# Gate and up of a gated feed-forward by seven half-size block products instead of eight, block sums on GpSimd

## The chip, the cores and the metric

One core of one Trainium2 chip runs the whole program. The metric is device time in microseconds (us). The engines are TensorE (PE, with its weight loads as PEld), VectorE (DVE), ScalarE (ACT), GpSimd (POOL) and SyncE (SP), which issues the loads of weights.

## What is computed

The reference is a stack of four layers on 512 tokens of width 1024, all in float32: two layers with a mixer, a cross attention to a memory, and a gated feed-forward; then two layers with another mixer and a feed-forward of squared ReLU. The change is in the gated one:

```python
D_FF = -(-(8 * D_MODEL) // (3 * 256)) * 256          # 2816
def swiglu_ffn(x, w_gate, w_up, w_down):
    return (jax.nn.silu(x @ w_gate) * (x @ w_up)) @ w_down
...
for l in range(DEPTH):                                # DEPTH = 2
    ...
    y = swiglu_ffn(x, ffn_wg[l], ffn_wu[l], ffn_wd[l])
    x = layer_norm(ALPHA * x + y, ln_ffn_g[l], ln_ffn_b[l])
```

## The kernel before

Activations lie feature-major: `xs` holds eight tiles (k) of 128 features by 512 tokens. A float32 product is made of three single-pass products: each operand is split into a high part (fp32r, written by ACT) and the rest (written by DVE), and `mm3` adds high*high, high*rest and rest*high in a PSUM bank. So every matmul of a product stands three times, each with its own weight load.

Weights come as units of 128 x 2048 floats (1 MB), in the order of their use. SP loads a unit into one of the two halves of `w_raw` when DVE has finished with the unit before in it; ACT writes the high part (`split_hi`, into `w_hi`) when PE is done with the unit before in that half, and DVE the rest (`split_lo`, into `w_lo`). Each engine has its own instruction stream, in order; all order between engines is by semaphores. PE runs the units in turn.

A gated feed-forward has 11 chunks of 256 hidden features. A chunk has three units: gate, up and down. `chunks("ffn0", ...)` and `chunks("ffn1", ...)` do on PE: gate and up of chunk 0; then ten times gate and up of chunk c (96 matmuls of 512 tokens) and down of chunk c-1 (48 of 512); then down of chunk 10. Gate and up each fill two PSUM banks (0 to 3) over eight k. ACT drains the gate with SiLU into `sil`, DVE multiplies it by up (`fh`), ACT and DVE split the product into `fhh` and `fhl` (L1622, L2258), and PE's down reads these. Down has eight output tiles, in banks 4 to 7 in turn; DVE adds each to `xs` (L2160), and tile m+4 can start only when tile m has been added. GpSimd computes nothing in this part. `scale_residual` (eight scalings of `xs` on DVE) stands beside the gate of chunk 0.

In all the trace's rows the matmuls have line 710 (`mm`), and the splits of units lines 1483 (ACT) and 2074 (DVE).

Of the kernel before, what the change touches and what calls it, by code (L numbers as in the profile page):

```python
# [30 lines left out]
KT = D // P  # L31
# [95 lines left out]
def plan_banks():  # L127
# [116 lines left out]
    def ups(name, tag, c, gated):  # L244
        f = []
        if gated:
            f += [((name, tag, "g", 0), 0, None), ((name, tag, "g", 1), 1, c)]
            c += 1
        b = 2 if gated else 2 * (side(UNITS[name]) ^ (tag != "first"))
        return f + [((name, tag, "u", 0), b, None), ((name, tag, "u", 1), b + 1, c)]  # L250
# [4 lines left out]
    def chunks(name, gated):  # L255
        c, k = UNITS[name], 2 if gated else 1
        for f in ups(name, "first", c, gated):
            fill(*f)
        c += k
        trips = LOOP_TRIPS[gated]  # L260
        loop(trips, 2 * (k + 1), ups(name, 0, c, gated) + downs(name, 0, c + k)
             + ups(name, 1, c + k + 1, gated) + downs(name, 1, c + 2 * k + 1))
        c += trips * 2 * (k + 1)
        if not gated:
            for f in ups(name, "late", c, gated) + downs(name, "late", c + k):
                fill(*f)
            c += k + 1
        for f in downs(name, "last", c):
            fill(*f)
# [6 lines left out]
    for l in range(2):  # L276
# [29 lines left out]
        chunks(f"ffn{l}", True)  # L306
# [13 lines left out]
    chunks("mlp0", False)  # L320
# [10 lines left out]
    chunks("mlp1", False)  # L331
# [3 lines left out]
LOOP_TRIPS = {True: (FFN_CHUNKS - 1) // 2, False: (MLP_CHUNKS - 2) // 2}  # L335
# [9 lines left out]
SO_FIRST = 12  # L345
plan_banks()


def slot(c):
    return (c + sum(s < c for s in SPARE)) % 2  # L350
# [30 lines left out]
class Seen:  # L381
# [14 lines left out]
SIGNALS = [  # L396
    "first_hi", "first_lo",
# [26 lines left out]
def build(nc, x, mem, params, consts, table, w_gk2, sinks, w, out):  # L424
    scratch = nc.dram_tensor("rel_scratch", [16, P, 384], F32, kind="Internal").ap()
    with ExitStack() as ctx:
# [8 lines left out]
        raw_loaded = [new_sem(f"raw_loaded{s}") for s in range(2)]  # L435
# [44 lines left out]
        sum_x = sb(ctx, "sum_x", [P, T])  # L480
        sum_q = sb(ctx, "sum_q", [P, T])
# [9 lines left out]
        meml = sb(first, "meml", [P, KT, MEM], F32R)  # L491
        mk = sb(first, "mk", [P, KT, MEM])
        vl0 = sb(alias, "vl0", [P, MT * D], F32R)
        alias.close()
# [18 lines left out]
        values_lo = [vl0, vl1]  # L513
        mv1 = sb(first, "mv1", [P, MT * D])
# [7 lines left out]
        sil = sb(ffn_mem, "sil", [P, 2, T])  # L522
        fh = sb(ffn_mem, "fh", [P, 2, T])
        fhh = sb(ffn_mem, "fhh", [P, 2, 2, T], F32R)
        fhl = sb(ffn_mem, "fhl", [P, 2, 2, T], F32R)
        ffn_mem.close()
# [28 lines left out]
        gb = sb(gla_mem, "gb", [P, HEADS, T])  # L555
        gk = sb(gla_mem, "gk", [P, HEADS, T])
# [7 lines left out]
        low_mem = ExitStack()  # L564
        glr_hi = sb(low_mem, "glr_hi", [P, KT * P], F32R)
        glr_lo = sb(low_mem, "glr_lo", [P, KT * P], F32R)
        low_mem.close()
# [15 lines left out]

        banks = [ctx.enter_context(nc.psum_tensor(f"bank{b}", [P, T], F32)) for b in range(8)]
# [4 lines left out]
        def wait_full(eng, key, i=None):  # L589

            b, _, _, unit, n, per = FILL[key]
            if unit is None:
                eng.wait_ge(bank_full[b], at(i, per, n))
            else:
                eng.wait_ge(unit_used, at(i, per, unit + 1))
# [24 lines left out]
        def last_down_keys(name):  # L620
            return [(name, "last", "d", m) for m in range(KT)]

        chunk_base = {"ffn0": 0, "ffn1": FFN_CHUNKS, "mlp0": 2 * FFN_CHUNKS, "mlp1": 2 * FFN_CHUNKS + MLP_CHUNKS}
        gated = {"ffn0": True, "ffn1": True, "mlp0": False, "mlp1": False}
# [5 lines left out]
        def _(sp):  # L630
            def load(s, n):
                sp.dma_start(w_raw[:, s, :], w[n, :, :]).then_inc(raw_loaded[s], 16)
# [10 lines left out]
            load(1, 1)  # L643
            with sp.Fori(1, N_UNITS // 2) as i:
                for s in range(2):
                    sp.wait_ge(w_lo_ready, i * 2 + (s - 1))
                    sp.dma_start(w_raw[:, s, :], w[bass.ds(i * 2 + s, 1), :, :].rearrange("a p n -> p (a n)"))\
                      .then_inc(raw_loaded[s], 16)
            if N_UNITS % 2:
                sp.wait_ge(w_lo_ready, N_UNITS - 2)  # L650
                load(0, N_UNITS - 1)
# [8 lines left out]
        def _(pool):  # L660
# [20 lines left out]
            pool.wait_ge(unit_used, UNITS["ffn0"] + 1)  # L681
            const(window[:, :, :, :].rearrange("p a g t -> p (a g t)"), "window", window_loaded)
            pool.wait_ge(unit_used, UNITS["glr"])
# [7 lines left out]
            pool.wait_ge(unit_used, UNITS["mlp0"])  # L691
            const(kk[0:33, 0, 0:384], "onehot", onehot_loaded, 33)
            wait_drained(pool, ("vec", 0))
            for g in range(8):
                heads = slice(2 * g, 2 * g + 2)
                pool.wait_ge(unit_used, UNITS["mlp0"] + 3 + 2 * g)
                pool.dma_start(scratch[heads, :, :], vt[heads, 0:384].unsqueeze(1).broadcast_to([2, P, 384])).then_inc(vec_stored, 16)
            pool.wait_ge(vec_stored, 8 * 16)
            for g in range(8):
                pool.wait_ge(unit_used, UNITS["mlp0"] + 20 + g)  # L700
# [5 lines left out]
        def _(pe):  # L706
# [29 lines left out]
            def feature_unit(stage, j, src=xtile, n=T, ready=None):  # L736

                c = UNITS[stage] + j
                if c:
                    pe.wait_ge(w_lo_ready, c + 1)  # L740
# [10 lines left out]
            def last_unit(stage, j, src=xtile):  # L751

                c = UNITS[stage] + j
                pe.wait_ge(w_lo_ready, c + 1)
# [6 lines left out]
            def token_half(stage, p, half, src, tiles):  # L761

                c = UNITS[stage] + 2 * p + half
                pe.wait_ge(w_lo_ready, c + 1)
# [93 lines left out]
            def keep_array_busy(key, c):  # L858

                pe.wait_ge(w_hi_ready, c + 1)  # L860
# [188 lines left out]
            def out_tiles(l, tiles):  # L1049
# [3 lines left out]
                if tiles[0] == 0:  # L1053
                    pe.wait_ge(w_lo_ready, c + 1)
# [53 lines left out]

            def chunks(name, ready):


                U, base, gate = UNITS[name], chunk_base[name], gated[name]
                hh, hl = (fhh, fhl) if gate else (mhh, mhl)
                src = xtile if gate else ytile
                k_ = 2 if gate else 1

                def up(tag, c, i=None, ready=None):
                    for which in ("g", "u") if gate else ("u",):
# [3 lines left out]
                        for k in range(KT):  # L1122
                            if ready:
                                ready(k)
# [1763 lines left out]
```

## Time and profile before

| | |
|---|---|
| time, median of 3 runs | 2422.66 us (2421.19 to 2422.84) |
| span of the profiled execution | 2419.9 us |
| its time around the span | not shown on the page; the median is 2.8 us above the span |
| PE busy | 2386.0 us, 99% |
| DVE, ACT, GpSimd busy | 1448.5, 873.7, 22.7 us |

The profile is one execution with hardware timestamps. Its page gives each engine's busy time and the chain of work that ended last; the trace behind it gives single instructions in order of time, groups of instructions with mean duration (one line per shape), busy times within stretches, and the DMA issues with their time to landing. A matmul's duration overlaps that of the next one, so what a matmul costs is read from the distance between two starts, not from its mean duration.

### The profile page before, as it was taken

How to read it: one execution, taken by the hardware profiler on the slowest of the kernel's cores; microseconds unless marked ns; L12 is line 12 of the kernel's file. 1: busy time of each engine (PE TensorE's matmuls, PEld its weight loads, DVE VectorE, ACT ScalarE, POOL GpSimd, SP SyncE). 2: the span in 40 equal slices, each digit the busy share in tenths (PEclk: the TensorE clock that was granted, in tenths of full speed). 3: DMA queues.
4: the chain of work that ended last, by engine and by line, in shares of the span. 5: the costliest groups of instructions: out<-in, count | busy, mean ns of one | idle time of the engine just before them, and what ended most of it. 6: DMA issues, size and time to landing. Idle time of an engine off the chain costs nothing.

```text
span 2419.9 us, 28651 instructions
## 1 busy us (share of the span) xinstructions
PE 2386.0 (99%) x11134; PEld 1944.4 (80%) x11134; DVE 1448.5 (60%) x1994; ACT 873.7 (36%) x1230; POOL 22.7 (1%) x39
## 2 busy tenths in 40 slices
PE   8999999999999999999999999999999999999998
PEld 7887888888887887888887786888888777888886
DVE  6997646444446846444446725565566776665566
ACT  4455445222223834322223625422122465222122
POOL 0000000000000000000000000000000000000000
PEclk9999999999999999999999999999999999999999
DMA  5222312322222211222222220233333211222221
GB/s 183 105 101 92 122 35 105 114 104 88 103 88 103 77 64 70 105 97 94 97 94 102 77 105 35 83 109 118 120 112 120 87 53 64 93 96 95 104 90 66
DMA packets 38811, 228.06 MB, mean 94 GB/s; under 512 B 8837, under 2 KB 8917, under 8 KB 12496
## 3 DMA queue, kind: packets, MB, share of 16 engines
q1 hardware_dynamic: 31680, 219.17, 25.3%
q0 software_dynamic: 7056, 7.86, 1.3%
q8 instruction: 52, 0.85, 0.1%
q14 instruction: 23, 0.19, 0.0%
HBM read 221.71 MB, written 5.24 MB: 94 GB/s over the span
## 4 chain that ended last, share of the span: by engine, by line
PE 86%; DVE 7%; ACT 5%; issue 1%; DMA 1%; SPq 0%; DVEq 0%; ACTq 0%
PE bank L710 85%; DVE w_lo L2074 2%; ACT w_hi L1483 1%; DMA w_raw<-weights_in 1%; ACT xs L1564 1%; ACT xh L1502 1%; DVE xl L2089 1%; DVE cacc L2310 1%; PE bank L1414 1%; DVE xs L2204 0%; DVE xs L2184 0%; ACT pr L1806 0%; DVE sum_x L2096 0%; DVE sum_q L2103 0%; DVE xs L2160 0%
## 5 line engine op out<-in xcount | busy, mean ns | idle before, releaser
L2074 DVE TENSOR_TENSOR w_lo<-w_raw,w_hi 128x2048 fp32r<-128x2048 f32 x200 | 458.2, 2291 | 372.7 <-ACT w_hi L1483 372.6
L710 PE MATMUL bank<-xh,w_hi 128*128 128x512 f32 x1408 | 553.6, 393 | 13.3 <-DVE w_lo L2532 6.7
L710 PE MATMUL bank<-xl,w_hi 128*128 128x512 f32 x1408 | 548.9, 390 | 0.0
L710 PE MATMUL bank<-xh,w_lo 128*128 128x512 f32 x1408 | 548.8, 390 | 0.0
L1483 ACT ACTIVATE w_hi<-w_raw 128x2048 fp32r<-128x2048 f32 x200 | 381.6, 1908 | 400.1 <-PE bank L710 394.1
L2160 DVE TENSOR_TENSOR xs<-xs,bank 128x512 f32<-128x512 f32 x448 | 294.5, 684 | 102.1 <-PE bank L710 101.1
L710 PEld LDWEIGHTS bank<-xh,w_hi 128*128 128x128 f32 x1408 | 264.8, 188 | 77.2 <-DVE w_lo L2532 6.7
L710 PEld LDWEIGHTS bank<-xh,w_lo 128*128 128x128 f32 x1408 | 264.8, 188 | 55.4
L710 PEld LDWEIGHTS bank<-xl,w_hi 128*128 128x128 f32 x1408 | 265.0, 188 | 54.3 <-issue 0.5
L710 PE MATMUL bank<-yh,w_hi 128*128 128x512 f32 x576 | 227.2, 394 | 0.4 <-DVE w_lo L2074 0.3
L710 PE MATMUL bank<-yl,w_hi 128*128 128x512 f32 x576 | 224.3, 389 | 0.0
L710 PE MATMUL bank<-yh,w_lo 128*128 128x512 f32 x576 | 224.2, 389 | 0.0
L710 PE MATMUL bank<-mhh,w_hi 128*128 128x512 f32 x512 | 199.2, 389 | 0.0
L710 PE MATMUL bank<-mhl,w_hi 128*128 128x512 f32 x512 | 199.2, 389 | 0.0
L710 PE MATMUL bank<-mhh,w_lo 128*128 128x512 f32 x512 | 199.2, 389 | 0.0
L1622 ACT ACTIVATE mhh<-mh 128x512 fp32r<-128x512 f32 x64 | 39.5, 633 | 312.9 <-DVE mh L2254 312.9
L2249 DVE TENSOR_TENSOR mh<-bank,rstd 128x512 f32<-128x512 f32 x64 | 43.7, 691 | 173.8 <-PE bank L710 173.8
L710 PE MATMUL bank<-fhh,w_hi 128*128 128x512 f32 x352 | 136.9, 389 | 0.0
L710 PE MATMUL bank<-fhl,w_hi 128*128 128x512 f32 x352 | 136.9, 389 | 0.0
L710 PE MATMUL bank<-fhh,w_lo 128*128 128x512 f32 x352 | 136.9, 389 | 0.0
L710 PEld LDWEIGHTS bank<-yh,w_hi 128*128 128x128 f32 x576 | 108.1, 188 | 28.5 <-issue 6.6
L710 PEld LDWEIGHTS bank<-yh,w_lo 128*128 128x128 f32 x576 | 108.1, 188 | 22.9
(299 smaller groups left out, 2868.3 us busy)
## 6 DMA issues: line engine op xcount, KB each, us to landing
w_raw<-weights_in SPq DMA_DIRECT2D x204, 1024.0 KB, 4.8
rel_scratch<-vt POOLq DMA_DIRECT2D x8, 384.0 KB, 19.9
bias<-rel_scratch POOLq DMA_DIRECT2D x8, 256.0 KB, 3.2
y_out<-xs SPq DMA_DIRECT2D x8, 256.0 KB, 2.2
xs<-x_in SPq DMA_DIRECT2D x3, 512.0 KB, 8.7
mk<-mem_in POOLq DMA_DIRECT2D x1, 1024.0 KB, 7.3
window<-consts_in POOLq DMA_DIRECT2D x1, 576.0 KB, 6.4
xs<-x_in SPq DMA_DIRECT2D x2, 256.0 KB, 4.5
```

The source lines that it names most:

```text
L710: return pe.matmul(dst, a, b, start=start, stop=stop)
L1414: last = pe.transpose(bank(key)[:, s_ * P:(s_ + 1) * P], pv[:, s_ * P:(s_ + 1) * P], ident[:, :])
L1483: act.activation(w_hi[:, slot(c), :], w_raw[:, c % 2, :], ACT.Copy).then_inc(w_hi_ready, 1)
L1502: give(act.activation((xh if dst is None else dst)[:, k, :], src, ACT.Copy, **kw), "x_hi")
L1564: give(act.activation(xs[:, k, :], xs[:, k, :], ACT.Identity, scale=col(f"{param}_g{l}", k), bias=col(f"{param}_b{l}", k)), "xn_ready")
L1622: give(act.activation(hh[:, chunk % 2, m, :], src, ACT.Copy), "hh_ready")
L2074: dve.tensor_tensor(w_lo[:, slot(c), :], w_raw[:, c % 2, :], w_hi[:, slot(c), :].bitcast(F32), ALU.subtract)\
L2089: return dve.tensor_tensor(l, src, h, ALU.subtract)
L2160: free(dve.tensor_tensor(xs[:, k, :], xs[:, k, :], bank(key)[:, :], ALU.add), key)
L2249: free(dve.tensor_tensor(hid[:, chunk % 2, m, :], bank(key)[:, :], rstd[:, :], ALU.mult), key)
L2310: ins = dve.scalar_tensor_tensor(a, u, wj, a, ALU.mult, ALU.add)
```

## The change

Chunk 0 of each gated layer stays as it was. For chunks 1 to 10, gate and up are computed by Strassen's scheme: the contraction (1024 features) is cut into halves (low, high), the tokens into halves (early, late) and the 256 hidden features into halves. Instead of eight products of such blocks there are seven, of sums of blocks. One product takes gate and up together (u = 0, 1 in the two halves of one bank): 2 x 4 k x 3 = 24 matmuls with 256 tokens, so 168 for a chunk. The order of the products is 2, 5, 1, 4, 3, 7, 6 of the token operands.

- Sums of weight blocks (five for each chunk, each 128 x 1024 floats) and of token blocks (five for each layer) are made by GpSimd, into two buffers (`sums`, `sq`) in turn; a sum waits until DVE has made the rest of the sum before last (`sum_parts`).
- ACT and DVE split seven half units for each chunk (`unit_part`, 128 x 1024 each) in place of two whole ones. The parts of products lie in a ring of three: the part of product n+3 can be written only when product n is done.
- Products come out of PSUM by three ACT copies and six DVE additions into `gu`, and two subtractions between quarters of it (`from_copies`). SiLU and the product with up then run in `gu`.
- The gate and up units of chunk c+1 overwrite `w_raw` when the last sum of chunk c has been made. Down units have a raw buffer of their own, and a single place in `w_hi` and `w_lo` (the other place is part of the ring): `split_hi` of a down unit waits until the down before it is done on PE.
- SP's loads and the gated layers' code are written out instead of looped. `scale_residual` moves behind the seventh part of chunk 1. The host packs gate and up weights in quarters (`quartered`).

```diff
--- before.py
+++ after.py
...
+        def ring(name, c, j):
+            g = (PRODUCTS * (c - 1) + j) % RING
+            if g == 0:
+                return ring_hi[:, :], ring_lo[:, :]
+            a, s = slice((g - 1) * UNIT // 2, g * UNIT // 2), 1 - W_SLOT[UNITS[name] + 1]
+            return w_hi[:, s, a], w_lo[:, s, a]
+
+        def quadrant(q):
+            return w_raw[:, :, q * T:(q + 1) * T]
+
+        def sum_of(key):
+            return (sq if SUM[key] % 2 else sums)[:, :, :]
...
+            for n in range(2, N_UNITS):
+                before = RAW_BEFORE[n]
+                if before in PAIRED:
+                    name, c = PAIRED[before]
+                    sp.wait_ge(sem["sum_made"], SUM[name, c, PRODUCTS - 1] + 1)
+                    sp.wait_ge(sem["part_lo"], PART[name, c, 1] + 1)
+                elif n in (down_unit("ffn0", 0), down_unit("ffn1", 0)):
+                    sp.wait_ge(unit_used, nth(n - 4) + 1)
+                else:
+                    sp.wait_ge(w_lo_ready, nth(before) + 1)
+                load(n)
...
+            def sum_parts(name, key, a, b, op):
+                t = SUM[key]
+                if t >= 2:
+                    pool.wait_ge(sem["part_lo"], SUM_PART[t - 2] + 1)
+                pool.tensor_tensor(sum_of(key), a, b, op).then_inc(sem["sum_made"], 1)
...
+            def gated_sums(name, norms):
+
+                pool.wait_ge(sem["xn_ready"], norms * KT)
+                sum_tokens(name, 2, (low, late), (high_, late), ALU.add)
+                sum_tokens(name, 5, (low, early), (high_, early), ALU.add)
+                sum_tokens(name, 1, (low, early), (high_, late), ALU.add)
+                for c in range(1, FFN_CHUNKS):
+                    for n in (UNITS[name] + 3 * c - 1, UNITS[name] + 3 * c):
+                        pool.wait_ge(raw_loaded[RAW_SLOT[n]], 16 * RAW_COUNT[n])
+                    sum_parts(name, (name, c, 2), quadrant(0), quadrant(3), ALU.add)
+                    sum_parts(name, (name, c, 3), quadrant(2), quadrant(0), ALU.subtract)
+                    if c == 1:
+                        sum_tokens(name, 7, (high_, early), (high_, late), ALU.subtract)
+                        sum_tokens(name, 6, (low, late), (low, early), ALU.subtract)
+                    sum_parts(name, (name, c, 4), quadrant(1), quadrant(3), ALU.subtract)
+                    sum_parts(name, (name, c, 5), quadrant(2), quadrant(3), ALU.add)
+                    sum_parts(name, (name, c, 6), quadrant(0), quadrant(1), ALU.add)
...
+                def product(c, j, s):
+                    key = (name, "p", c, j)
+                    pe.wait_ge(sem["part_lo"], PART[name, c, j] + 1)
+                    wait_free(pe, key)
+                    wh, wl = ring(name, c, j)
+                    h, l = operand(s)
+                    for u in range(2):
+                        for k in range(KT // 2):
+                            a = slice(u * T + k * P, u * T + (k + 1) * P)
+                            last = mm3(bank(key)[:, u * 256:(u + 1) * 256], (wh[:, a], wl[:, a]), (h[:, k, :], l[:, k, :]),
+                                       k == 0, k == KT // 2 - 1)
+                    full(last, key)
+
+                whole("g", UNITS[name], ready)
+                whole("u", UNITS[name] + 1)
+                for c in range(1, FFN_CHUNKS):
+                    for j, s in enumerate((2, 5, 1, 4, 3, 7, 6)):
+                        product(c, j, s)
+                    down(name, c - 1, down_unit(name, c - 1), c - 1)
+                down(name, FFN_CHUNKS - 1, down_unit(name, FFN_CHUNKS - 1), FFN_CHUNKS - 1)
...
+                if c - 1 in DOWNS and c not in DOWNS and i is None:
+                    act.wait_ge(unit_used, nth(c - 1))
+                elif W_BEFORE[c] is not None:
+                    act.wait_ge(unit_used, at(i, per, nth(W_BEFORE[c]) + 1))
+                act.activation(w_hi[:, slot(c), :], raw(c), ACT.Copy).then_inc(w_hi_ready, 1)
...
+                def unit_part(c, j):
+                    key = (name, c, j)
+                    g = PRODUCTS * (c - 1) + j
+                    if g >= RING:
+                        before = (g - RING) // PRODUCTS + 1, (g - RING) % PRODUCTS
+                        wait_full(act, (name, "p", *before))
+                    elif g:
+                        act.wait_ge(unit_used, nth(U) + (own_slot == W_SLOT.get(U)))
+                    if j >= 2:
+                        act.wait_ge(sem["sum_made"], SUM[key] + 1)
+                        src = sum_of(key)
+                    else:
+                        for n in (U + 3 * c - 1, U + 3 * c):
+                            act.wait_ge(raw_loaded[RAW_SLOT[n]], 16 * RAW_COUNT[n])
+                        src = quadrant(3 * j)
+                    give(act.activation(ring(name, c, j)[0].rearrange("p (u n) -> p u n", u=2), src, ACT.Copy), "part_hi")
...
+                def gate(c, f):
+
+                    for j in ((3, 5), (4, 6))[f]:
+                        wait_drained(act, (name, "p", c, j))
+                    g = gu[:, gate_side(name, c), f, :]
+                    give(act.activation(g, g, ACT.Silu), "sil_ready")
...
+                for c in range(1, FFN_CHUNKS):
+                    act.wait_ge(sem["h_ready"], 2 * (base + c))
+                    product_out(c, 0, 0, late)
+                    unit_part(c, 3)
+                    split_hi(down_unit(name, c - 1))
+                    if c == 1:
+                        act.wait_ge(unit_used, nth(U + 1) + 1)
+                        for s in (7, 6):
+                            token_part(s)
+                    product_out(c, 1, 1, early)
+                    unit_part(c, 4)
+                    product_out(c, 2, 0, early)
+                    unit_part(c, 5)
+                    unit_part(c, 6)
+                    if c + 1 < FFN_CHUNKS:
+                        unit_part(c + 1, 0)
+                        unit_part(c + 1, 1)
+                    gate(c, 0)
+                    if c + 1 < FFN_CHUNKS:
+                        unit_part(c + 1, 2)
+                    gate(c, 1)
+                    for m in range(2):
+                        hidden(c, m)
+                split_hi(down_unit(name, FFN_CHUNKS - 1))
...
+                def from_copies(c):
+
+                    for j in range(3):
+                        wait_drained(dve, (name, "p", c, j))
+                    steps.step(dve.tensor_tensor(quarter(1, late), quarter(0, early), quarter(0, late), ALU.subtract))
+                    steps.step(dve.tensor_tensor(quarter(0, early), quarter(0, early), quarter(1, early), ALU.subtract))
+
+                def add_to_two(c, j, first, second):
+
+                    wait_full(dve, (name, "p", c, j))
+                    steps.wait()
+                    steps.step(add_product(c, j, *first))
+                    free(add_product(c, j, *second), (name, "p", c, j))
+
+                def add_to_one(c, j, f, t, behind):
+                    wait_full(dve, (name, "p", c, j))
+                    steps.wait()
+                    wait_drained(dve, (name, "p", c, behind))
+                    free(add_product(c, j, f, t), (name, "p", c, j))
...
+                for s in (2, 5, 1):
+                    token_part(s)
+                for j in range(RING):
+                    unit_part(1, j)
+                for m in range(2):
+                    first_hidden(m)
+                for m in range(2):
+                    rest_of_hidden(0, m)
+                for c in range(1, FFN_CHUNKS):
+                    unit_part(c, 3)
+                    if c == 1:
+                        for s in (7, 6):
+                            token_part(s)
+                    split_lo(down_unit(name, c - 1))
+                    unit_part(c, 4)
+                    from_copies(c)
+                    unit_part(c, 5)
+                    add_to_two(c, 3, (0, early), (0, late))
+                    unit_part(c, 6)
+                    if c == 1:
+                        dve.wait_ge(sem["sum_made"], SUM[name, "x", 6] + 1)
+                        scale_residual()
+                    add_to_two(c, 4, (1, early), (1, late))
+                    if c + 1 < FFN_CHUNKS:
+                        unit_part(c + 1, 0)
+                    add_to_one(c, 5, 0, early, 3)
+                    if c + 1 < FFN_CHUNKS:
+                        unit_part(c + 1, 1)
+                    add_to_one(c, 6, 1, late, 4)
+                    hidden(c, 0)
+                    down(c - 1, range(0, 2))
+                    hidden(c, 1)
+                    down(c - 1, range(2, 3))
+                    if c + 1 < FFN_CHUNKS:
+                        unit_part(c + 1, 2)
+                    down(c - 1, range(3, 5))
+                    rest_of_hidden(c, 0)
+                    down(c - 1, range(5, 6))
+                    rest_of_hidden(c, 1)
+                    down(c - 1, range(6, KT))
+                split_lo(down_unit(name, FFN_CHUNKS - 1))
+                keys = last_down_keys(name)
+                for k in range(KT):
+                    add(k, keys[k])
+                    sums_between(k, keys, True)
```

## Rows read from the trace of the kernel before

**Rows 1.** The page: busy times, and granted clock of PE over 40 slices.

```profile
PE 2386.0 (99%) x11134; PEld 1944.4 (80%) x11134; DVE 1448.5 (60%) x1994; ACT 873.7 (36%) x1230; POOL 22.7 (1%) x39
...
PEclk9999999999999999999999999999999999999999
```

**Rows 2.** Chain that ended last, one stretch: start, us, what.

```profile
999.96 66.19 PE bank L710 x292
```

**Rows 3.** Windows: two passes of the loop of chunks.

```profile
core 0: us, PE busy (x) PEld busy (x) DVE busy (x) ACT busy (x) POOL busy (x), PEclk, DMA share, GB/s
1000.00:1065.24 65.24, 65.24 (x289) 54.03 (x288) 29.19 (x30) 15.92 (x14) 0.00 (x0) 1.00 0.27 97
```

**Rows 4.** Timeline of PE, 512 tokens: start, us; first and last of 24.

```profile
391.66 0.39 PE L710 MATMUL bank<-xh,w_hi 128*128 128x512 f32 x1
...
396.87 0.40 PE L710 MATMUL bank<-xh,w_lo 128*128 128x512 f32 x1
```

**Rows 5.** Timeline of PE, 256 tokens: first and last of 47.

```profile
145.40 0.28 PE L710 MATMUL bank<-meml,w_hi 128*128 128x256 f32 x1
...
150.92 0.28 PE L710 MATMUL bank<-memh,w_lo 128*128 128x256 f32 x1
```

**Rows 6.** Groups of DVE: busy us, mean ns; idle before.

```profile
line engine op names shapes xcount | busy us, mean ns | idle before us <-releasers
L2074 DVE TENSOR_TENSOR w_lo<-w_raw,w_hi 128x2048 fp32r<-128x2048 f32 x200 | 458.2, 2291 | 372.7 <-ACT w_hi L1483 372.6
L2160 DVE TENSOR_TENSOR xs<-xs,bank 128x512 f32<-128x512 f32 x448 | 294.5, 684 | 102.1 <-PE bank L710 101.1
...
L2258 DVE TENSOR_TENSOR fhl<-fh,fhh 128x512 fp32r<-128x512 f32 x44 | 28.6, 690 | 2.2
L2247 DVE TENSOR_TENSOR fh<-sil,bank 128x512 f32<-128x512 f32 x44 | 28.3, 685 | 118.4 <-PE bank L710 111.2 <-issue 7.2
...
L2224 DVE TENSOR_SCALAR xs<-xs 128x512 f32<-128x512 f32 x16 | 5.5, 422 | 0.0
...
L2522 DVE TENSOR_TENSOR vl<-mv,vh 128x1024 fp32r<-128x1024 f32 x4 | 4.9, 1218 | 0.0
```

**Rows 7.** Groups of ACT.

```profile
L1483 ACT ACTIVATE w_hi<-w_raw 128x2048 fp32r<-128x2048 f32 x200 | 381.6, 1908 | 400.1 <-PE bank L710 394.1 <-DMA w_raw<-weights_in 6.0
...
L1622 ACT ACTIVATE fhh<-fh 128x512 fp32r<-128x512 f32 x44 | 27.1, 633 | 190.8 <-DVE fh L2247 190.8
L1488 ACT ACTIVATE sil<-bank 128x512 f32<-128x512 f32 x44 | 26.3, 598 | 165.6 <-PE bank L710 163.8
...
L1801 ACT ACTIVATE vh<-mv 128x1024 fp32r<-128x1024 f32 x4 | 4.2, 1047 | 0.0
```

**Rows 8.** Groups of GpSimd: its largest compute operation and a smallest.

```profile
L667 POOL MEMSET ones<- 128x128 f32 x1 | 0.2, 205 | 0.0
...
L666 POOL MEMSET eps<- 128x1 f32 x1 | 0.1, 98 | 0.3 <-POOLq L2878 0.3
```

**Rows 9.** DMA issues: count, KB each, median us to landing.

```profile
w_raw<-weights_in SPq DMA_DIRECT2D x204, 1024.0 KB, 4.8
```

**Rows 10.** Windows within one load: DMA share, GB/s.

```profile
core 0: us, , PEclk, DMA share, GB/s
1012.00:1013.00 1.00, 1.00 0.76 221
1013.00:1014.00 1.00, 1.00 0.92 369
1014.00:1015.00 1.00, 1.00 0.94 393
1015.00:1016.00 1.00, 1.00 0.16 66
```

**Rows 11.** Timeline of DVE in one chunk.

```profile
1013.59 0.69 DVE L2160 TENSOR_TENSOR xs<-xs,bank 128x512 f32<-128x512 f32 x1 [0.67 <-PE bank L710]
...
1029.63 2.29 DVE L2074 TENSOR_TENSOR w_lo<-w_raw,w_hi 128x2048 fp32r<-128x2048 f32 x1 [9.07 <-ACT w_hi L1483]
```

**Rows 12.** Waits: who waited for whom.

```profile
ACT w_hi L1483 <- PE bank L710: 394.1, 60, 9.4
DVE w_lo L2074 <- ACT w_hi L1483: 372.6, 121, 9.4
```

More of the change, by code:

```diff
@@ L642, in _ @@
                 sp.dma_start(xs[:, 2 * c:2 * c + 2, :], x[:, 2 * c:2 * c + 2, :]).then_inc(x_loaded[c + 1], 16)
[L643 to L651, printed above, removed]
+            load(1)
+            for n in range(2, N_UNITS):
[9 more added lines that the diff above has]
+                load(n)
             for k in range(KT):
@@ L1107, in cross_attention, with down @@
                 return step
+            def down(name, tag, c, chunk, i=None, per=0):
+                hh, hl = (fhh, fhl) if name[:3] == "ffn" else (mhh, mhl)
+                pe.wait_ge(w_lo_ready, at(i, per, nth(c) + 1))
+                pe.wait_ge(sem["h_ready"], at(i, 4, 2 * (chunk_base[name] + chunk) + 2))
+                for m in range(KT):
+                    key = (name, tag, "d", m)
+                    wait_free(pe, key, i)
+                    for k in range(2):
+                        last = mm3(bank(key)[:, :], weights(c, k * D + m * P, P),
+                                   (hh[:, chunk % 2, k, :], hl[:, chunk % 2, k, :]), k == 0, k == 1)
+                    full(last, key)
@@ L1133, in down @@
-                def down(tag, c, chunk, i=None):
-                    pe.wait_ge(w_lo_ready, at(i, per, c + 1))
-                    pe.wait_ge(sem["h_ready"], at(i, 4, 2 * (base + chunk) + 2))
-                    for m in range(KT):
-                        key = (name, tag, "d", m)
-                        wait_free(pe, key, i)
-                        for k in range(2):
-                            last = mm3(bank(key)[:, :], weights(c, k * D + m * P, P),
-                                       (hh[:, chunk % 2, k, :], hl[:, chunk % 2, k, :]), k == 0, k == 1)
-                        full(last, key)
@@ L1146, in chunks @@
+                per = 4
                 up("first", U, ready=ready)
-                c = U + k_
-                with pe.Fori(0, trips) as i:
+                c = U + 1
+                with pe.Fori(0, MLP_TRIPS) as i:
                     up(0, c, i)
-                    down(0, c + k_, 0, i)
-                    up(1, c + k_ + 1, i)
-                    down(1, c + 2 * k_ + 1, 1, i)
-                c += trips * per
-                if not gate:
-                    up("late", c)
-                    down("late", c + k_, 2 * trips)
-                    c += k_ + 1
```

482 lines of the change are left out of this document (304 added, 178 removed).

## Prediction, made before the change was run

> **What bounds the kernel.** I read the page first. PE is busy 99% of the span at the full granted clock, DVE 60%, ACT 36%, GpSimd 1% [rows 1]. The chain of work that ended last is nothing but PE in the middle of a gated layer: one piece of 66.19 us with 292 matmuls [rows 2]. The windows over one pass of the loop of chunks (two chunks) say the same: PE has no gap in 65.24 us, DVE works 29.19 and ACT 15.92 [rows 3]. The waits are those of ACT for PE and of DVE for ACT, not of PE [rows 12], and DVE stands idle for 9.07 us ahead of one split [rows 11]. So only PE's matmuls count before, and whatever delays PE afterwards counts in full.
>
> What does a matmul cost? Its duration (0.39 us) overlaps the next one's. The distance of starts is what counts: 24 matmuls of 512 tokens start from 391.66 to 396.87, which is 5.21 / 23 = 0.2265 us [rows 4]; 47 of 256 tokens from 145.40 to 150.92, which is 5.52 / 46 = 0.120 us [rows 5]. Half the tokens cost 53%, not 50%: about 13 ns of each matmul does not scale. A chunk of 144 matmuls of 512 then takes 32.62 us, and two of them 65.24, as in [rows 3].
>
> **What PE saves.** Gate and up of a chunk: 96 x 0.2265 = 21.74 us before, 168 x 0.120 = 20.16 after. One eighth less arithmetic would be 2.7 us; the fixed part of 72 more matmuls takes back 1.1 of it. 1.58 us are left, so 31.7 us for 20 chunks, and a chunk without waits takes 20.16 + 48 x 0.2265 = 31.03 us. This is the whole gain. All the rest of the change can only cost.
>
> **What is added for each chunk.** ACT: seven half units at 1.05 in place of two whole ones at 1.91, the down unit 1.91, three copies from PSUM at 0.60, two SiLU and two splits at 0.63 [rows 7]: some 13.6 us. DVE: seven rests at 1.22, the down unit 2.29, six additions from PSUM at 0.69, two subtractions, two products and two rests at 0.69, eight additions into the residual at 0.68 [rows 6]: 24.5 us. Both are below 31.03, but now in a fixed order with short deadlines. GpSimd: five sums of 1024 floats a partition. No row shows a sum on GpSimd. Its largest operation, a fill of 128 x 128, takes 205 ns and a tiny one 98 [rows 8], so 0.84 ns per float. Lower bound: as fast as DVE, 1.22 us [rows 6]. Two streams of operands in turn at the fill's price give 0.1 + 2 x 0.86 = 1.8 us, three streams (the write too) 2.7, which I take as the upper bound with 2.8. I take 2.3, between the two. The Trainium skill, GPSIMD Engine Reference, section Performance versus the Vector engine, gives 4497 ns for a sum of 2048 floats; half of that would be 2.25, and the sum the same.
>
> **The schedule of a middle chunk**, with 0 at the start of its first product (2.88 us each: products end at 2.88, 5.76, 8.64, 11.52, 14.40, 17.28, 20.16; down tiles of 1.36 follow to 31.03). Part 3 can be written when product 0 is done: ACT copies the product (to 3.6), writes the high part (4.65), DVE the rest (5.9). ACT then writes the high part of the down unit (6.6), DVE its rest (8.95), and only behind it stands the rest of part 4: 10.2, with its product due at 11.5. GpSimd may begin the last sum of the chunk only then, and only when that is made may SP load the next chunk's gate and up. A load lands 4.8 us after its issue [rows 9]; while it moves, it moves 370 to 390 GB/s [rows 10], so a second one of 1.05 MB lands 2.7 us behind it, together 7.4. Parts 0 and 1 of the next chunk wait for both, and in DVE's stream these stand ahead of the last two product additions, these ahead of the hidden product, and this ahead of the addition of down tile 0. Down tile 4 needs the bank of tile 0 and is due at 25.6.
>
> *Side by side*, GpSimd and DVE not disturbing each other: last sum 12.55, both units landed 20.0, rest of part 0 at 22.35, addition 23.05, rest of part 1 at 24.25, addition 24.95, hidden product 25.65, tile 0 added 26.35. PE waits 0.8 us. Everything else is in time.
>
> *In turn*: a GpSimd sum, which reads two tensors of SBUF, and a DVE operation with two inputs in SBUF never run together, and whoever asked first goes first. Which of the two holds, no row shows: GpSimd never computes here while DVE works [rows 1, 8]. The sum set off by part 3 then runs 5.9 to 8.25, and the down unit's rest waits for it: 10.6. Part 4 comes at 11.85, 0.4 late. The subtractions of `from_copies` and the last sum take turns: sum done at 14.9, subtractions 15.6, part 5 at 16.85 against product 4's end at 14.8: PE waits 2.1. Loads are issued at 15.0 and landed at 22.4. The sum that they release runs to 24.75, the rest of part 0 waits for it: 25.95; another sum to 28.25, part 1 at 29.5, last addition 30.2, hidden product 30.9, tile 0 added 31.6, where tile 4 was due at 28.1: 3.5. Together 6.0 us of waits, so a chunk of 37.05 against 32.62. I forecast this case. The Trainium skill speaks against the change here: in SBUF — State Buffer, section Who interferes with whom, a DVE instruction with two SBUF inputs contends with a GpSimd instruction that reads SBUF, under an exclusive lock. By that rule the case in turn holds; no row of this trace bears on it.
>
> **First and last chunks.** In chunk 1 of each layer two more token sums and their parts stand ahead of parts 3 to 5, and `scale_residual` (8 x 0.42 [rows 6]) in DVE's stream. The same working gives part 4 at 14.0 side by side (2.5 late) and the loads some 3.7 later (1.9 more at tile 4): 4.4 us; in turn, part 4 at 18.8 (7.3 late), part 5 2.0 late, tile 4 3.5 late: 12.8. Chunk 10 has no parts of a next one: 2.5 in turn, nothing side by side. Behind it, the last down unit can be split only when the down before it is done, since down units now have one place. Its cover is gone: ACT 1.91 and DVE 2.29 with the hand-over lie bare, 4.3 us for each layer in both cases. Token sums and parts for chunk 1 (some 12 us on GpSimd) lie under gate and up of chunk 0 (21.7 us of PE); SP's longer code, and the repacking, cost nothing, as each load is some 2.7 us of moving in a chunk of over 30.
>
> **The sum** is made against the profiled span, 2419.9; the median is 2.8 above it and I add the same. In turn: 16 middle chunks x 6.0 = 96.0, chunk 1 2 x 12.8 = 25.6, chunk 10 2 x 2.5 = 5.0, last down 2 x 4.3 = 8.6, less 31.7: +103.5. So 2419.9 + 103.5 + 2.8 = 2526 us.
>
> **Rivals.** (1) Side by side: 16 x 0.8 + 2 x 4.4 + 8.6 - 31.7 = -1.5, so 2421: no change. For it: DVE's 24.5 us and ACT's 13.6 fit easily. Against: nothing in the rows; it hangs on the one open question. (2) Faster: side by side, and a GpSimd sum at DVE's price, 1.22. The second unit then lands at 18.9 and tile 0 is added before 25.6. Waits are left in chunk 1 (2 us each) and at the last down: 4.0 + 8.6 - 31.7 = -19.1, so 2404. It decides from the point at which the second unit lands by 19.2. (3) In turn with cheap sums (1.22): part 5 0.25 late and tile 4 1.25 late, 16 x 1.5 + 14 + 0.5 + 8.6 - 31.7 = +15, so 2438. (4) In turn with dear sums (2.8): part 4 0.85, part 5 2.5 and tile 4 4.4 late, 16 x 7.75 + 30 + 6.8 + 8.6 - 31.7 = +138, so 2561; if DVE's next operation goes ahead of a waiting sum, the loads come later by 1.8 and it is +26 on the forecast, 2552. Each microsecond of a sum is worth about 60 us in this case, since two sums and the loads stand in one chain.
>
> **How the numbers follow.** The forecast with its neighbours, sums between some 1.9 and 2.6 us in turn (2490 to 2550): 0.55. Dearer (4): 0.13. Cheap in turn (3), up to 2490: 0.08. Side by side (1), 2414 to 2430: 0.13. Faster (2): 0.11. The range of 8 in 10 runs from 2416, inside case 1, to 2562, the upper bound. A measurement of this kernel can tell about 0.2% (4.8 us) from no change. Faster has case 2 and a part of case 1: 0.14; same most of case 1: 0.10; slower the rest: 0.76.
>
> **What would show it.** Starts of product matmuls 0.120 us apart and 24 to a product; the mean of a GpSimd sum against 2.3 us; DVE's `unit_part` rests longer than 1.22 us, or gaps ahead of them, whenever a sum runs; gaps of PE ahead of product 5 and down tile 4 in each chunk, and 4.3 us ahead of the last down; chunks some 37 us apart. I am wrong if the sums and DVE's splits overlap in the timeline with neither longer, if the two loads land sooner than 7.4 us after their issue, or if a matmul of 256 tokens with strided operands isn't 0.120. PE's short gaps should leave the granted clock at full; if the clock falls in the 4.3 us gap, some microseconds are added.

## The result, and the profile after

The changed kernel takes 2562.45 us (2560.58 to 2564.53, 4 runs) against 2421.93 us before on the same chip: ratio 1.058, with a 95% interval of 1.0565 to 1.0595. It is slower by 140.5 us. The forecast was 2526 (+103.5 us of the profiled span), with a range up to 2562. The direction and the mechanism held; the size did not: the time is 36 us above the forecast and just above the range.

The page of the changed kernel, with the lines that answer to [rows 1], and the chain by line:

```profile
span 2558.5 us, 31229 instructions
...
PE 2408.7 (94%) x12574; PEld 2015.5 (79%) x12574; DVE 1793.5 (70%) x2264; ACT 980.2 (38%) x1400; POOL 321.7 (13%) x149
...
PE bank L867 63%; DMA w_raw<-weights_in 6%; DVE w_lo L2320 4%; ACT w_hi L1667 2%; DVE w_lo L2540 2%; DVE ring_lo L2540 1%; ACT w_hi L1836 1%; POOL sums L807 1%; POOL sq L807 1%; DVE gu L2548 1%; DVE xl L2335 1%; ACT xs L1748 1%; ACT xh L1686 1%; DVE xs L2406 1%; ACT ring_hi L1836 1%
```

PE is busy for about as long as before, 2408.7 against 2386.0, but in a longer span; its share falls from 99% to 94%. The chain is no longer PE alone: loads, splits and sums stand in it.

The chain through one middle chunk (start, us, what; product 0 starts at 600.60):

```profile
604.22 1.05 ACT w_hi L1836
605.28 1.81 ACT w_hi L1667
...
607.11 3.01 DVE w_lo L2320
...
611.10 1.22 DVE w_lo L2540
...
612.38 2.79 POOL sq L807
...
615.61 6.79 DMA w_raw<-weights_in
...
622.50 1.07 ACT w_hi L1836
...
626.60 2.75 DVE ring_lo L2540
629.35 0.60 DVE gu L2548
629.95 0.60 DVE gu L2573
630.55 0.61 DVE xs L2406
...
631.20 1.22 PE bank L867 x2
```

This is step for step the schedule of the prediction: high part of the down unit, its rest, part 4, the last sum, two loads, parts of the next chunk, a product's addition, the hidden product, tile 0, and only then tile 4. Both loads have landed 7.2 us after the first was issued (615.19); in the first layer's middle chunks it is 7.2 to 7.8 us, and 7.4 was forecast. Tile 0 is added 30.6 us after the chunk's start; 31.6 was forecast.

The timeline of DVE and that of GpSimd in the same chunk:

```profile
612.83 2.88 DVE L2555 TENSOR_TENSOR gu<-gu 128x512 f32<-128x512 f32 x1
...
625.93 0.68 DVE L2548 TENSOR_TENSOR gu<-gu,bank 128x512 f32<-128x512 f32 x1
626.53 2.82 DVE L2540 TENSOR_TENSOR ring_lo<-w_raw,ring_hi 128x1024 fp32r<-128x1024 f32 x1
```

```profile
606.61 2.41 POOL L807 TENSOR_TENSOR sums<-w_raw 128x1024 f32<-128x1024 f32 x1 [7.70 <-DVE w_lo L2540]
612.38 2.78 POOL L807 TENSOR_TENSOR sq<-w_raw 128x1024 f32<-128x1024 f32 x1 [3.36 <-DVE w_lo L2540]
622.52 2.40 POOL L807 TENSOR_TENSOR sums<-w_raw 128x1024 f32<-128x1024 f32 x1 [7.36 <-DMA w_raw<-weights_in]
624.88 3.39 POOL L807 TENSOR_TENSOR sq<-w_raw 128x1024 f32<-128x1024 f32 x1
```

These lines show who holds whom. The subtraction at 612.83, an operation of 0.68 us, takes 2.88, because a sum has begun at 612.38; it ends 0.55 us behind that sum's end. The sum at 624.88 takes 3.39 instead of 2.40, because DVE's rest of 2.41 us (from 623.60) still runs to 626.0. The addition at 625.93, which reads one operand from PSUM, takes 0.68 us with a sum in flight. This is the case "in turn".

What the prediction did not price is the clock. Windows around the wait ahead of tile 4 (PE's busy time, then granted clock as a share of 2.4 GHz):

```profile
core 0: us, PE busy (x), PEclk, DMA share, GB/s
...
624.00:628.00 4.00, 4.00 (x20) 1.00 0.05 16
628.00:632.00 4.00, 1.18 (x4) 0.86 0.00 0
632.00:636.00 4.00, 4.00 (x14) 0.72 0.00 0
636.00:640.00 4.00, 4.00 (x27) 1.00 0.00 0
```

Behind a stretch in which PE stood for over 3 us, it works at 1.2 GHz instead of 2.4 for part of the down tiles. 14 and 27 matmuls start in the two 4 us after the wait, where the full clock gives some 17.7 down matmuls. (The second of these windows also holds product matmuls, which are shorter.) The trace's clock records show the same behind the wait ahead of tile 4 in all 16 middle chunks: 3.4 us at half clock in 13 of them, 6.8 us in the other three.

### The profile page after: what moved, and what is told of

Its sections match the earlier page's. It is cut to its first block, busy times and chain, and to the rows that moved or that the text cites. A ratio compares the mean times of both kernels' runs of the same rounds, so it can differ in the third digit from the quotient of the medians.

```text
span 2558.5 us, 31229 instructions
## 1 busy us (share of the span) xinstructions
PE 2408.7 (94%) x12574; PEld 2015.5 (79%) x12574; DVE 1793.5 (70%) x2264; ACT 980.2 (38%) x1400; POOL 321.7 (13%) x149
## 4 chain that ended last, share of the span: by engine, by line
PE 64%; DVE 16%; ACT 7%; DMA 6%; issue 4%; POOL 2%; SPq 0%; DVEq 0%; ACTq 0%
PE bank L867 63%; DMA w_raw<-weights_in 6%; DVE w_lo L2320 4%; ACT w_hi L1667 2%; DVE w_lo L2540 2%; DVE ring_lo L2540 1%; ACT w_hi L1836 1%; POOL sums L807 1%; POOL sq L807 1%; DVE gu L2548 1%; DVE xl L2335 1%; ACT xs L1748 1%; ACT xh L1686 1%; DVE xs L2406 1%; ACT ring_hi L1836 1%
## 5 line engine op out<-in xcount | busy, mean ns | idle before, releaser
L867 PE MATMUL bank<-xh,w_hi 128*128 128x512 f32 (+1 forms) x1184 | 428.4, 362 | 55.4 <-DVE w_lo L2540 34.9
L2320 DVE TENSOR_TENSOR w_lo<-w_raw,w_hi 128x2048 fp32r<-128x2048 f32 x138 | 320.4, 2322 | 164.7 <-ACT w_hi L1667 164.6
L867 PE MATMUL bank<-xl,w_hi 128*128 128x512 f32 (+1 forms) x1184 | 420.0, 355 | 0.0
L867 PE MATMUL bank<-xh,w_lo 128*128 128x512 f32 (+1 forms) x1184 | 419.9, 355 | 0.0
L1667 ACT ACTIVATE w_hi<-w_raw 128x2048 fp32r<-128x2048 f32 x138 | 263.2, 1907 | 253.1 <-PE bank L867 247.5
L867 PEld LDWEIGHTS bank<-xh,w_hi 128*128 128x128 f32 x1184 | 226.6, 191 | 100.5 <-DVE w_lo L2540 41.3
L867 PEld LDWEIGHTS bank<-xh,w_lo 128*128 128x128 f32 x1184 | 226.5, 191 | 30.8
L867 PEld LDWEIGHTS bank<-xl,w_hi 128*128 128x128 f32 x1184 | 227.0, 192 | 29.5 <-issue 0.5
L807 POOL TENSOR_TENSOR sums<-w_raw 128x1024 f32<-128x1024 f32 x50 | 136.7, 2733 | 226.0 <-DVE w_lo L2540 103.3
L807 POOL TENSOR_TENSOR sq<-w_raw 128x1024 f32<-128x1024 f32 x50 | 136.7, 2733 | 225.9 <-DVE w_lo L2540 102.8
```

Source lines behind the costliest of these rows:

```text
L807: pool.tensor_tensor(sum_of(key), a, b, op).then_inc(sem["sum_made"], 1)
L867: return pe.matmul(dst, a, b, start=start, stop=stop)
L1667: act.activation(w_hi[:, slot(c), :], raw(c), ACT.Copy).then_inc(w_hi_ready, 1)
L2320: dve.tensor_tensor(w_lo[:, slot(c), :], raw(c), w_hi[:, slot(c), :].bitcast(F32), ALU.subtract)\
```

## The experiments

Ten kernels, each timed against the kernel before on the same chip. Ratios are to it.

**Sums without reading: long and short fills.** These take the reading away from GpSimd and nearly leave its length, then cut the length too. The sums themselves are left out; token sums are changed like the weight sums shown here.

```diff
-                pool.tensor_tensor(sum_of(key), a, b, op).then_inc(sem["sum_made"], 1)
+                for k_fill in range(2):
+                    pool.memset(sum_of(key), 0.01).then_inc(pool_steps, 1)
+                    fills[0] += 1
+                    pool.wait_ge(pool_steps, fills[0])
+                pool.memset(sum_of(key)[:, 0, 0:256], 0.01).then_inc(sem["sum_made"], 1)
```

> The kernel after, but each GpSimd sum is replaced by fills of its buffer that take about as long (2.4 us) and read nothing; the blocks' sums are left out. Theory A (a sum and a DVE operation with two SBUF inputs take turns): the waits of DVE go, all its rests are 1.22 us long, a middle chunk is about 32 us, in all 2420 to 2435 us. Rival B (the sum's own length in the chain to the loads is what costs, DVE isn't held up): nothing changes, 2555 to 2565 us.

> As the write-only run, but with one fill of about 1 us for each sum. Theory A: the second load lands 1.4 us earlier than with the long fills and tile 4 is in time in the middle chunks, 2400 to 2412 us. Rival B: 2562 less 1.4 us for two sums in the chain of each of 18 chunks, 2505 to 2515 us.

Measured: 2421.39 us with the long fills (ratio 0.9997, 0.9988 to 1.0007), 2409.83 with the short ones (0.9943, 0.9927 to 0.996). Groups of DVE, first of the changed kernel, then with the long fills:

```profile
L2320 DVE TENSOR_TENSOR w_lo<-d_raw,w_hi 128x2048 fp32r<-128x2048 f32 x22 | 86.5, 3934 | 13.0 <-ACT w_hi L1667 13.0
...
L2540 DVE TENSOR_TENSOR w_lo<-w_raw,w_hi 128x1024 fp32r<-128x1024 f32 x26 | 69.7, 2680 | 36.2 <-ACT w_hi L1836 36.2
L2555 DVE TENSOR_TENSOR gu<-gu 128x512 f32<-128x512 f32 x20 | 57.6, 2882 | 0.0
```

```profile
L2330 DVE TENSOR_TENSOR w_lo<-d_raw,w_hi 128x2048 fp32r<-128x2048 f32 x22 | 50.4, 2292 | 13.0 <-ACT w_hi L1677 13.0
...
L2550 DVE TENSOR_TENSOR w_lo<-w_raw,w_hi 128x1024 fp32r<-128x1024 f32 x26 | 31.8, 1222 | 56.9 <-ACT w_hi L1846 56.9
...
L2565 DVE TENSOR_TENSOR gu<-gu 128x512 f32<-128x512 f32 x20 | 13.7, 684 | 0.0
```

3934, 2680 and 2882 ns become 2292, 1222 and 684. Three fills in a row take GpSimd 2.34 us, a sum that nothing holds 2.40; so the 141 us hang on GpSimd's reading of SBUF at the same time as DVE, and on what follows from it (the granted clock is 0.979 with the sums and 0.997 with the fills), not on how long GpSimd is at work. With the long fills the time is the one forecast for "side by side" (2421). With the short ones a middle chunk takes PE's bare 31.06 us (31.03 forecast), two in these windows (busy times, clock):

```profile
562.12:624.24 62.12, 62.12 (x433) 58.33 (x432) 44.54 (x56) 25.57 (x30) 9.44 (x10) 1.00 0.26 103
```

So theory A holds and B falls. Rival 2 of the prediction, forecast at 2404 with sums of 1.22 us, comes nearest to the short fills of 0.957; it is 6 us below them.

**The gap ahead of tile 4 filled.** The wait stays, but PE isn't idle in it.

```diff
+                    if m == 4 and name[:3] == "ffn" and chunk + 2 < FFN_CHUNKS:
+                        nxt = (name, "p", chunk + 2, 0)
+                        wait_free(pe, nxt)
+                        for _ in range(24):
+                            mm(bank(nxt)[:, 0:256], x2h[:, 0, 0:P], x2h[:, 0, :], True, True)
                     wait_free(pe, key, i)
```

> The kernel after with 24 idle matmuls of 256 tokens (2.9 us) ahead of down tile 4 of each chunk but the last two, into the bank of the next product, where PE stands for 3.2 us. Theory D (the idle stretch takes the clock to half for 3.4 us, and that costs 1.7 us or more in each chunk): 2525 to 2535 us, with the granted clock at full in the middle chunks. If the half clock costs nothing beside the waits: 2558 to 2566 us.

Measured: 2533.66 us (1.0457, 1.044 to 1.0475), 29 us less with 432 matmuls more. The mean granted clock over the run rises from 0.979 to 0.992, no middle chunk has half clock any more, and a middle chunk takes 36.5 us on average instead of 38.2. So the half clock behind this wait costs about 29 us.

**Additions first.** DVE's and ACT's queues in another order; the DVE side:

```diff
                     add_to_two(c, 4, (1, early), (1, late))
-                    if c + 1 < FFN_CHUNKS:
-                        unit_part(c + 1, 0)
                     add_to_one(c, 5, 0, early, 3)
-                    if c + 1 < FFN_CHUNKS:
-                        unit_part(c + 1, 1)
                     add_to_one(c, 6, 1, late, 4)
                     hidden(c, 0)
                     down(c - 1, range(0, 2))
                     hidden(c, 1)
                     down(c - 1, range(2, 3))
+                    # then parts 0, 1, 2 of c + 1 between the other down tiles
```

> The kernel after in another order on ACT and DVE: the last product additions, SiLU, the hidden product and the addition of down tiles 0 to 2 stand ahead of parts 0 to 2 of the next chunk, instead of parts 0 and 1 ahead of them. Theory A (tile 4 waits for a load that stands ahead of tile 0's addition in DVE's queue): the wait of 3.2 us ahead of tile 4 and the half clock behind it (1.7 us) go in each of 18 chunks, 2465 to 2480 us. Rival C (DVE and GpSimd in turn are simply full, so the wait only moves to another place): 2540 to 2562 us.

Measured: 2479.14 us (1.0231, 1.0214 to 1.0248), 83 us less, one of the largest effects of the study, from an order alone. A middle chunk takes 33.5 us at full clock. The wait ahead of tile 4 is gone, those ahead of products 4 and 5 (0.6 and 1.6) remain.

**Parts first**, on top of it, in DVE's queue:

```diff
                     unit_part(c, 4)
-                    from_copies(c)
                     unit_part(c, 5)
-                    add_to_two(c, 3, (0, early), (0, late))
+                    from_copies(c)
                     unit_part(c, 6)
+                    add_to_two(c, 3, (0, early), (0, late))
```

> The kernel with the additions first, and now part 5 ahead of from_copies and part 6 ahead of the addition of product 3 on DVE. Theory A (product 5 waits 1.5 us since from_copies, held up by the last sum, stands ahead of part 5): the wait goes in 20 chunks and at most 0.4 us of it comes back at product 6, 2448 to 2460 us. Rival C (DVE and GpSimd in turn are full): 2472 to 2480 us.

Measured: 2458.29 us (1.0156, 1.0139 to 1.0173). Within the expectation.

**Another place for the last down unit**, on top of it:

```diff
         s = last_down if n in DOWNS else nxt
+        if n in (down_unit("ffn0", FFN_CHUNKS - 1), down_unit("ffn1", FFN_CHUNKS - 1)):
+            s = 1 - last_down
```

> As the kernel with parts first, and the last down unit of each layer goes to the other place of w_hi and w_lo, so it needn't wait for the down before it. Theory A: the gap of 4.5 us ahead of the last down and the half clock behind it go, twice: 9 to 14 us less than with parts first.

Measured: 2453.98 us (1.0131), 4 us less, a miss. The gap ahead of the last down shrinks only from 4.5 to 3.1 us: its split now needn't wait for the place, but in DVE's queue it stands behind the additions of the down before. Half clock still follows it in both layers.

**Parts ahead of the down unit's split**, on top of it. ACT's queue moves alike; in chunk 1 GpSimd's token sums 7 and 6 each go one weight sum later. DVE's side:

```diff
                     unit_part(c, 3)
-                    if c == 1:
-                        for s in (7, 6):
-                            token_part(s)
-                    split_lo(down_unit(name, c - 1))
                     unit_part(c, 4)
+                    if c == 1:
+                        token_part(7)
                     unit_part(c, 5)
-                    from_copies(c)
+                    if c == 1:
+                        token_part(6)
+                    split_lo(down_unit(name, c - 1))
                     unit_part(c, 6)
+                    from_copies(c)
```

> As the kernel with the last down unit's place; and parts 3 to 5 stand ahead of the down unit's split (2.3 us on DVE) and part 6 ahead of from_copies; in chunk 1 the two token sums and their parts come behind parts 4 and 5 instead of ahead of part 4. Theory A (every wait of PE comes from the order of DVE's queue, not from its load): PE waits under 0.5 us in a middle chunk and 3 us in chunk 1, in all 2405 to 2420 us, at or below the time before the change. Rival C (24.5 us of DVE and five sums of 2.4 in turn nearly fill 31 us): the waits come back at the down tiles or at product 3, 2425 to 2445 us.

Measured: 2445.16 us (1.0092, 1.0075 to 1.0109), above the 2405 to 2420 expected and at the rival's upper end. But the windows show where: first two middle chunks, then chunk 1 of the first layer (busy of PE, PEld, DVE, ACT, GpSimd).

```profile
580.05:642.17 62.12, 62.12 (x433) 58.28 (x432) 55.26 (x57) 25.47 (x30) 24.90 (x10) 1.00 0.26 103
442.87:486.81 43.94, 34.72 (x218) 31.62 (x216) 39.54 (x37) 16.17 (x19) 17.97 (x7) 0.92 0.19 72
```

These two middle chunks have no wait of PE at all, with ten sums of two inputs in 62 us and DVE busy 55.26 of it, the time of being held included; all 16 take 31.2 us on average, the longest 32.2. So the load in turn fits and theory A is right there. Chunk 1 (43.94 us) still waits. There token sums and weight sums stand in one queue of GpSimd; that this chain is what makes it long is argued, and the next two runs bear on it.

**Token sums later**, on top of it: they wait for the up unit's rest.

```diff
                 pool.wait_ge(sem["xn_ready"], norms * KT)
+                pool.wait_ge(w_lo_ready, nth(UNITS[name] + 1) + 1)
                 sum_tokens(name, 2, (low, late), (high_, late), ALU.add)
```

> As the kernel with parts ahead, and the token sums of a layer start only when the rest of the up unit of chunk 0 has been made. Theory A (two token sums in flight hold up that rest by 2.2 us, and PE waits 2.9 us ahead of up): 4 to 8 us less than with parts ahead. If the later token sums then hold up the first products: no gain.

Measured: 2447.49 us (1.0106), no gain. In the first layer the first product starts 25.6 us behind its gate instead of 29.2, but chunk 1 ends no sooner (49.3 us instead of 43.9). Taking one wait away only moves it.

**Token sums on DVE**, without that wait, the residual scaled by ACT, and the last down's split ahead of DVE's last additions. DVE's side in short:

```diff
+                token_sum(2)
+                token_sum(5)
+                token_part(2)
+                token_sum(1)
+                token_part(5)
+                token_part(1)
...
-                    if c == 1:
-                        dve.wait_ge(sem["sum_made"], SUM[name, "x", 6] + 1)
-                        scale_residual()
...
+                    if c == FFN_CHUNKS - 1:
+                        split_lo(down_unit(name, c))
                     down(c - 1, range(6, KT))
-                split_lo(down_unit(name, FFN_CHUNKS - 1))
```

> As the kernel with parts ahead; the five token sums of a layer are made by DVE (1.22 us each) instead of GpSimd, the residual is scaled by ACT in chunk 1 instead of DVE, and DVE splits the last down unit ahead of its last two additions of the down before. Theory A (what is left, 23 us above the time before the change, is the chain of sums and parts in turn through chunks 0 and 1, 7 and 13 us for a layer, and 3.4 us at the last down): 25 to 35 us less than with parts ahead, 2410 to 2420 us, level with or just below the time before. If the sums of weights alone make chunks 0 and 1 as long: 2438 to 2446 us.

Measured: 2415.22 us over 8 runs, ratio 0.9973 (0.9963 to 0.9984). This is faster than the kernel before, by 6 us, and 147 us faster than the change as it was made. Its mean granted clock is 0.996. The run has several edits at once, and the two traces say where its 30 us against "parts ahead" lie: chunk 0 is 12 us shorter in the two layers together (22.5 and 23.8 us, from 29.2 in both), chunk 1 9 us, chunk 10 with the last down 10 us (the gap ahead of the last down is 1.0 instead of 3.1, with no half clock behind it). Chunk 1 still takes 40.8 and 40.6 us; what holds it there was not tested.

**One operand instead of two**, in the kernel as it was changed. The sums hold one of their operands alone; token sums are changed alike.

```diff
-                pool.tensor_tensor(sum_of(key), a, b, op).then_inc(sem["sum_made"], 1)
+                pool.tensor_scalar(sum_of(key), a, 1.0, None, ALU.mult).then_inc(sem["sum_made"], 1)
```

> The kernel after with each sum replaced by GpSimd reading only its first operand and writing it (a multiplication by 1), so one SBUF input instead of two; the sums are left out. If any reading of SBUF by GpSimd takes turns with DVE's operations of two SBUF inputs: DVE's rests still come out longer than 1.22 us where they meet, and with a length of 1.1 to 1.8 us for each such operation the time lies between 2420 and 2510 us. If only two-input operations of GpSimd do: rests of 1.22 us throughout and a time like that of the fills of like length, 2408 to 2422 us.

Measured: 2478.39 us (1.024, 1.0224 to 1.0257). The time lies in the range for "any reading of SBUF by GpSimd takes turns", but the operation was longer than I expected, 2.77 us. Timelines of GpSimd and DVE in one stretch:

```profile
616.68 2.78 POOL L807 TENSOR_SCALAR sq<-w_raw 128x1024 f32<-128x1024 f32 x1 [5.86 <-DVE w_lo L2540]
...
632.08 2.78 POOL L807 TENSOR_SCALAR sq<-w_raw 128x1024 f32<-128x1024 f32 x1 [7.86 <-DMA w_raw<-weights_in]
634.83 2.77 POOL L807 TENSOR_SCALAR sums<-w_raw 128x1024 f32<-128x1024 f32 x1
```

```profile
617.17 2.69 DVE L2320 TENSOR_TENSOR w_lo<-d_raw,w_hi 128x2048 fp32r<-128x2048 f32 x1 [0.58 <-ACT w_hi L1667]
...
633.15 1.23 DVE L2540 TENSOR_TENSOR ring_lo<-w_raw,ring_hi 128x1024 fp32r<-128x1024 f32 x1 [5.31 <-ACT ring_hi L1836]
...
634.89 2.05 DVE L2540 TENSOR_TENSOR w_lo<-w_raw,w_hi 128x1024 fp32r<-128x1024 f32 x1
```

A rest of 1.22 us begun 0.06 us behind GpSimd's takes 2.05, so 0.83 longer, and is over before GpSimd is done. The down split, begun 0.49 us behind, takes 0.40 longer than its 2.29. Both say that DVE is held for the first 0.9 us of the 2.77. The rest at 633.15 fits: it begins 1.07 us behind GpSimd's operation and takes its plain 1.23, with 1.7 us of that operation still to run. With two operands DVE was held nearly to the end. So one operand takes turns too, but only for a third of its length.

## What in the prediction was right, and which step of it failed

The direction, the wait and the path were right. The step that failed is a term that the sum put at nothing: "PE's short gaps should leave the granted clock at full". They did not, and the half clock cost about 39 us where the sum fell short by 36. The terms one by one:

**PE's saving** was right: matmuls of 256 tokens start 0.120 us apart, and without GpSimd's reading a chunk takes 31.06 us.

**The mechanism** was right, and was the open question: sums and DVE's operations with two SBUF inputs take turns. The Trainium skill, SBUF — State Buffer, section Who interferes with whom, says that they contend under an exclusive lock, and the traces agree (2.88 us for a subtraction of 0.68). The chain from part 4 over sum and loads to tile 4 is the one forecast.

**A GpSimd sum** was taken as 2.3 us, between bounds of 1.22 and 2.8. It is 2.40 us where nothing holds it; the mean with holding is:

```profile
L807 POOL TENSOR_TENSOR sums<-w_raw 128x1024 f32<-128x1024 f32 x50 | 136.7, 2733 | 226.0 <-DVE w_lo L2540 103.3
```

Taking 2.3 for 2.40 is worth 6 us by the forecast's own 60 us for each microsecond; the waits nonetheless came out shorter.

**The middle chunks**: the 16 take 38.2 us on average (304.6 + 307.1 us in all), 37.05 were forecast, +19. Their waits are smaller than forecast: 1.6 ahead of product 5 instead of 2.1, 0.25 instead of 0.4 ahead of product 4, 3.0 to 3.5 ahead of tile 4 in most and 3.8 and 4.7 in two; 5.1 in all, for 6.0. What makes the chunks longer is the clock. Windows of the changed kernel over chunk 1, the eight middle chunks, and chunk 10 with the last down, in the first layer (length, PE's busy time, granted clock):

```profile
442.08:486.77 44.69, 33.65 (x217) 0.89 0.18 71
486.77:791.37 304.60, 268.58 (x1729) 0.95 0.21 84
791.37:841.68 50.31, 44.42 (x265) 0.97 0.20 75
```

The second layer's clocks are 0.89, 0.94 and 0.97. Behind these means the clock records show 65 us at half clock in the 16 middle chunks. PE works in 61 of them and loses half, 30 us, and the filled gap gives back 29. Counted in the same way, chunk 1 loses 4 us in the two layers together, chunk 10 with the last down 3, and chunk 0 of the first layer 2: 39 us in all.

**Chunk 0** was another term put at nothing: I hid the token sums "under gate and up of chunk 0". PE time is there, but two token sums hold up the rest of the up unit (4.46 us instead of 2.29), and PE waits 2.9 us ahead of up. Product 0 starts 27.9 and 27.6 us after the gate in the two layers. Before the change this stretch was 22.5 and 23.8 us: +5 and +4, the 2 us of clock included.

**Chunk 1** took 44.7 and 46.5 us, 13.7 and 15.5 over the bare 31.03, where 12.8 was forecast: +4, which is its 4 us of half clock. Its waits lie elsewhere than forecast: 8.8 and 9.5 us ahead of product 4 (7.3 forecast), none ahead of product 5 (2.0). **Chunk 10 and the last down** came out at 8.2 us a layer over PE's work, forecast 6.8: +3, and 3 us is the clock's part. These five differences add up to 19 + 5 + 4 + 4 + 3 = 35 us, and the profiled +138.6 lies 35 over the forecast +103.5. By cause it is some 39 us of clock and 7 us of waits in chunk 0, less 12 us of waits in the middle chunks that were priced too high: nearly the same 35. That the clock alone nearly equals what was missing is in part luck: two other errors nearly cancel.

**The rivals.** "Side by side" was worked out well (2421, and 2421.39 with the long fills) but doesn't hold on the chip. "In turn with dear sums" gives 2561, 1.5 us from the measured time, by a coincidence: it has 7.75 us of waits in a middle chunk, and 5.1 were there. What kept the measured time out of the range was that its upper end took in a longer sum but no loss of clock.

## What to carry to other kernels

Before work is moved to GpSimd, count what DVE reads from SBUF at the same time: the added engine isn't a free one, and each sum stops DVE's two-input operations for nearly its whole length. The cost then depends on the order of DVE's queue more than on the load: with the same sums a middle chunk took 38.2 us in one order and 31.2 in another, where what PE needs next stood first. And the waits of PE of 3 us and more are priced with the half clock behind them, here 1.5 to 1.7 us for most and 3 for some. Last, a change that saves one eighth of the arithmetic of gate and up saved 7% of PE's time on it (a middle chunk took 31.06 us instead of 32.62, 1.56 of the 21.74 us of its gate and up), since a matmul of half the tokens costs 53% of the whole one, not 50%.

## What the runs showed of the hardware

- A GpSimd sum of 128 x 1024 floats takes 2.40 us; a fill of the same size 0.957 us; one operand times a constant 2.77 us.
- GpSimd's fills do not hold DVE at all (rests of 1222 ns with fills in flight). Its operation with one SBUF input holds DVE's two-input operations for the first 0.9 us of 2.77. The Trainium skill, SBUF — State Buffer, section Summary: rules for kernel authors, has the second one fully blocked until the first finishes; for the one-input operation the trace differs, and the measurement decides.
- DVE's additions with one operand in PSUM take 675 ns on average in the changed kernel, and no longer with a sum in flight (0.68 us at 625.93), so sums don't touch them.
- In all 16 middle chunks of the changed kernel, where PE waits 3.0 us or more ahead of tile 4, the granted clock is at half (1.2 GHz) behind the wait for 3.4 or 6.8 us. With the long fills five middle chunks have waits of 0.7 to 1.6 us at the same place, and the clock stays at full.
